# Moving one tile's transposes and norms inside the layer-1 out-projection of a two-layer trunk kernel

## The reference, cut to what matters

```
for each layer:
    sh1, sc1, g1, sh2, sc2, g2 = split(silu(cond) @ w_ada + b_ada)      # one set for the prompt, one for the sample
    h = rms_norm(x, g_norm1) * (1 + sc1) + sh1
    y = mixer(h) @ w_o            # layer 0: gated MLP and windowed attention; layer 1: latent attention, 16 heads
    x = x + g1 * y
    h = rms_norm(x, g_norm2) * (1 + sc2) + sh2
    x = x + g2 * hier_moe(h)      # 32 experts of width 256, 2 per token, chosen by a router
```

## Time and profile before

| what | value |
|---|---|
| median of 3 runs (lowest, highest) | 1056.43 us (1052.93, 1058.72) |
| the profiled execution's own time | 1052.93 us |
| its span in the trace | 1051.1 us |
| PE busy | 904.6 us, 86% of the span |
| DVE busy | 399.2 us, 38% |
| ACT busy | 239.1 us, 23% |
| POOL busy | 120.9 us, 12% |
| chain that ended last: PE, DMA, DVE, ACT | 60%, 24%, 10%, 3% |

### The profile page before, as it was taken

The page is one execution under the profiler, slowest core; times in us unless marked ns, Lnnn a source line. Parts: engine busy times, 40 slices in busy tenths (PEclk is TensorE's granted clock), DMA queues, the critical chain, the costliest instruction groups (busy, mean ns, idle before and its releaser), DMA issues.

```text
span 1051.1 us, 14384 instructions
## 1 busy us (share of the span) xinstructions
PE 904.6 (86%) x5389; PEld 518.8 (49%) x5389; DVE 399.2 (38%) x1155; ACT 239.1 (23%) x598; POOL 120.9 (12%) x131
## 2 busy tenths in 40 slices
PE   4899788995899988998769997998869998889880
PEld 1345336555555544555346663554555554545550
DVE  1102366234622233221163574662654222522114
ACT  3110134111011111111244444433201111111111
POOL 1000000100122212121100000001001222121210
PEclk9999999895999999999979998999879999999995
DMA  9979799357698999999761028107799899999974
GB/s 379 397 275 409 295 419 398 97 200 244 228 362 345 411 415 415 390 414 413 273 256 46 1 84 338 70 1 255 258 414 351 315 408 416 416 404 414 414 304 186
DMA packets 68717, 318.72 MB, mean 303 GB/s; under 512 B 12470, under 2 KB 13494, under 8 KB 45992
## 3 DMA queue, kind: packets, MB, share of 16 engines
q1 hardware_dynamic: 53184, 285.84, 68.5%
q0 software_dynamic: 13328, 25.02, 7.0%
q10 hardware_dynamic: 2144, 7.05, 1.7%
HBM read 312.72 MB, written 26.49 MB: 323 GB/s over the span
## 4 chain that ended last, share of the span: by engine, by line
PE 60%; DMA 24%; DVE 10%; ACT 3%; issue 2%; SPq 1%; POOL 0%; POOLq 0%; DVEq 0%; ACTq 0%
DMA ring<-in_l_w 17%; PE psum L783 13%; PE psum L986 7%; PE psum L796 7%; PE psum L733 4%; DMA ring<-in_l_w_ada 3%; PE psum L1203 3%; PE psum L1101 2%; PE psum L1042 2%; PE psum L1092 2%; PE psum L624 2%; PE psum L763 2%; PE psum L1133 2%; DMA scratch<-token_rows_hbm,overflow_rows 2%; PE psum L746 1%
## 5 line engine op out<-in xcount | busy, mean ns | idle before, releaser
L783 PE MATMUL psum<-ring,scratch 128*64 128x256 f32 x1920 | 225.4, 388 | 30.3 <-DMA ring<-in_l_w 28.7
L783 PEld LDWEIGHTS psum<-ring,scratch 128*64 128x64 f32 x1920 | 144.7, 139 | 96.0 <-issue 41.2
L1980 DVE TENSOR_TENSOR scratch<-scratch,psum 64x256 f32<-64x256 f32 x64 | 27.2, 425 | 306.6 <-ACT scratch L1350 302.3
L796 PE MATMUL psum<-ring,scratch 128*64 128x512 f32 x496 | 119.9, 604 | 2.6 <-ACT scratch L1354 1.9
L2437 POOL DMA_INDIRECT expert_rows<-scratch,slot_rows x64 | 63.9, 999 | 342.6 <-ACT scratch L1364 336.8
L1350 ACT ACTIVATE scratch<-psum 64x256 f32<-64x256 f32 x64 | 24.1, 377 | 265.5 <-PE psum L783 252.6
L986 PE MATMUL psum<-ring,scratch 128*128 128x512 f32 x192 | 74.8, 549 | 1.3 <-DVE scratch L2113 1.3
L1364 ACT COPY scratch<-psum 128x512 f32<-128x512 f32 x64 | 37.5, 587 | 145.4 <-PE psum L796 145.4
L624 PE MATMUL psum<-ring,scT 128*32 128x512 f32 x320 | 42.7, 657 | 15.8 <-DMA ring<-in_l_w_ada 14.7
L986 PEld LDWEIGHTS psum<-ring,scratch 128*128 128x128 f32 x192 | 36.8, 194 | 37.6 <-issue 36.5
L796 PEld LDWEIGHTS psum<-ring,scratch 128*64 128x64 f32 x496 | 31.2, 136 | 44.8 <-issue 39.8
(11 more groups left out here) (341 smaller groups left out, 1130.4 us busy)
## 6 DMA issues: line engine op xcount, KB each, us to landing
ring<-in_l_w SPq DMA_DIRECT2D x180, 1024.0 KB
ring<-in_l_w_ada SPq DMA_DIRECT2D x48, 1024.0 KB, 5.2
ring<-in_l_w_o SPq DMA_DIRECT2D x8, 1024.0 KB
ring<-in_l_w_in SPq DMA_DIRECT2D x4, 1024.0 KB
gate_rows<-gate_rows_hbm POOLq DMA_DIRECT2D x8, 512.0 KB, 7.4
scale_shift<-gate_rows_hbm POOLq DMA_DIRECT2D x8, 512.0 KB, 10.7
scratch<-expert_rows SPq DMA_DIRECT2D x8, 512.0 KB, 5.3
ring<-in_l_w_in SPq DMA_DIRECT2D x4, 768.0 KB
```

What stands on the lines that cost most here:

```text
L783: last = nc.tensor.matmul(ps[64 * n:64 * n + 64, 2 + par, 0:DE], mine[:, k, :], part(w, k * DE, DE), start=k == 0, stop=k == KD - 1)
L796: last = nc.tensor.matmul(ps[64 * n:64 * n + 64, 5 + par, :], hhT[:, par, k, :], part(w2, k * D + n * 512, 512), start=k == 0, stop=k == 1)
```

## The change

Nothing is computed otherwise. Two engines get another order in layer 1.

```diff
@@ PE
             weighted_values1(len(ATT1) - 1)
             project_sample(1)
+            transpose_h(3, hp, 0)
             project_sample(2)
-            transpose_h(3, hp, 0)
             transpose_h(3, hp, 1)
             router(1)
@@ DVE
             evac_out1(len(ATT1) - 1)
+            norm(3, 0)
             residual_sample(1)
-            norm(3, 0)
+            evac_h(3, h2T, 0)
             norm(3, 1)
+            evac_h(3, h2T, 1)
             residual_sample(2)
-            evac_h(3, h2T, 0)
-            evac_h(3, h2T, 1)
             norm(3, 2)
             evac_h(3, h2T, 2)
             router(1)
```

## The result

| what | before | changed |
|---|---|---|
| median, us (lowest, highest) | 1056.43 (1052.93, 1058.72) | 1066.03 (1061.56, 1070.63) |
| ratio to before, 95% interval | | 1.0105 [1.0079, 1.0132] |
| span of the profiled execution | 1051.1 | 1065.9 |

The change makes the kernel slower by 8.3 to 13.9 us. The changed kernel was measured a second time, with 1.0115 [1.0089, 1.0142]. The forecast of 1069.9 lies 3.9 us above the median and inside its range, and its 13.5 us lie inside the first interval, near the upper end. The two spans lie 14.8 us apart, more than the medians: 13.5 us of this arise in the stage, and 1.35 us are a later start of the out-projection, ahead of the change.

The account below looks back on a forecast made before the run. PE alone bounds the out-projection, then a relay starting with the residual of tile 2. Terms 8.7 + 0.95 + 2.2 + 1.7 = 13.5 us on the median 1056.43 give 1069.9 us; range 1063 to 1075 for 8 in 10.

Parts of the forecast that it names:

- The wait on PE: Between the out-projection's halves PE stops for tile 0's norm, which waits for scale and shift rows: 8.7 us, bounds 2.4 to 10.7.
- The transposes: Tile 0's eight transposes now stand ahead of the out-projection's second half on PE: 0.95 us.
- The clock: PE's clock falls to 1.2 GHz in the stop and stays low for 4.4 us afterwards: 2.2 us, bounds 0 to 2.6.
- The copies ahead of the residual: Tile 1's transposes and DVE's copy now precede the residual of tile 2: 1.7 us, bounds 1.5 to 2.0.
- The sum: Four terms delay the residual of tile 2 by 13.5 us, bounds 4.9 to 16.2.
- The rest gives nothing back: After the residual of tile 2, router and experts recover none of the 13.5 us; no gain counted.
- my bound: Sign in the expert stage: wrong on the weights' stream if PE's waits for weights fall by more than 3 us.
- The rule against it: Skill's GpSimd transfer estimate for the scale and shift rows: landed about 6.8 us after issue, no stop, sum 2.65 us.
- A (rows in time): Scale and shift rows land as in layer 0 or faster, shrinking PE's stop: say 4 us, 1060.4 us; chance 0.06.
- B (the stream pays back): Experts' waits for weights shrink by up to 13.5 us: 1056.4 us, chance 0.03; half of it 1063, chance 0.05.
- C (the clock holds): No clock fall in PE's stop: 11.3 us, 1067.7 us; chance 0.82 together with the forecast.
- D: SP's seven later ring loads delay expert 1, or low clock reaches the logits: up to 5 us more, 1075; chance 0.04.

Follow-up runs that it names:

- e4: Changed kernel plus nine unused 512-column matmuls in PE's stop, ahead of tile 0's transposes; stage 38.77 us, ratio to before 1.0113 [1.0068, 1.0158].
- e3: Changed kernel, but SP starts layer 1's five early expert loads only after the scale and shift rows landed; stage 37.20 us, ratio to before 1.0086.
- e1: Kernel before with only PE's part of the change, DVE in its old order; stage 39.55 us, ratio to before 1.0123 [1.0074, 1.0173].
- e9: Changed kernel unaltered, second profile and second comparison with before; stage 41.19 us, ratio to before 1.0115 [1.0089, 1.0142].
- e5: Changed kernel with tile 0's transposes moved inside the out-projection's second half, before its seventh of eight steps; stage 33.04 us, ratio to before 1.0036.
- e6: Kernel before plus 15 unused 512-column matmuls between the out-projection's halves; stage 42.62 us, ratio to before 1.0169 [1.0133, 1.0206].
- e8: As e7, plus eight unused matmuls ahead of layer 1's first transposes; stage 29.68 us, ratio to before 0.9963 [0.9934, 0.9992].
- e10: Kernel before unaltered, second profile; stage 27.84 us, ratio to before 0.9993 [0.9971, 1.0016].
- e7: Kernel before plus unused 512-column matmuls behind both routers' logits, three in layer 1, two in layer 0; ratio to before 0.9968 [0.9944, 0.9993].
- e2: Kernel before with only DVE's part of the change, PE in its old order; stage 35.47 us, ratio to before 1.0076 [1.0051, 1.0101].

## Why the prediction was right

The terms are read from start to start, with e4 for what the clock did: the stage of 41.32 us is 22.34 to the first transposes, 1.76 to the second half, 15.46 to the next transposes and 1.76 to the residual.

- *The wait on PE*, 8.7 us forecast: 8.34 us of idle time, and 8.55 us from start to start (22.34 less 13.79, half of the old block). The rows landed 15.9 us after their issue (16.0 in before), and the norm went no earlier though it now stood first. Right. e3 shows that 4.4 us of the landing go away with SP's loads and that 11.5 us do not; the lower bound of the term, 2.4 us by layer 0's landing, was too low for this place, where 3.97 was found.
- *The transposes*, 0.95 us: in e4, at the high clock, 0.93 us from their start to that of the second half. Right.
- *The clock*, 2.2 us: 2.55 us between the stages of the changed kernel and e4, 0.83 in the transposes and 1.72 in the second half. Right in mechanism, 0.3 us small. The clock fell 3.3 us into the idle time and not 4.7, and in e3 a stop of 4 us had it.
- *The copies ahead of the residual*, 1.7 us: 1.49 us, at the lower bound. The 1.77 us between the changed kernel and e1 look closer to the forecast, but hold 0.28 us of a shorter wait and a shorter second half in e1. Right in mechanism, 0.2 us large.
- *The sum*, 13.5 us in the stage: 13.48 us. That it agrees within 0.02 us is luck: the clock came out 0.3 us larger, the wait and the copies some 0.2 us smaller each. In the whole kernel 11.1 us [8.3, 13.9] and on the repeat 12.1 us [9.4, 15.0], whose centres lie 2.4 and 1.4 us under the forecast. Whether this is a difference can't be said from these intervals. e9 shows one thing that would make a part of it: a low clock at the end of attention, seen in 4 of 12 profiles (e5, e6, e8, e9), costs 1.8 us in before and nothing in the changed kernel. At that frequency it is some 0.6 us on average, an estimate from twelve profiles of ten kernels.
- *The rest gives nothing back.* The tails, 298.08 and 298.03 us, and e6 bear it out. PE's waits for weights in the late part fell from 14.6 us in 11 waits to 12.1 in 8. They are no good sign either way: in the second profiles they are 16.3 us (before, e10) and 15.1 us (changed, e9), so one kernel's value moves by up to 3 us, which is all of my bound.

```profile
...
PE psum L783 <- DMA ring<-in_l_w: 12.1, 8, 3.0
...
```

The fall to 12.1 has a cause of its own, and it is not the delay of 13.5 us. The same group of products, before and then changed:

```profile
...
931.61 3.67 PE L783 MATMUL psum<-ring,scale_shift 128*64 128x256 f32 x32 [0.92 <-DVE scale_shift L2056]
...
```

```profile
...
946.48 6.61 PE L783 MATMUL psum<-ring,scale_shift 128*64 128x256 f32 x32 [0.92 <-DVE scale_shift L2056]
...
```

Counted from the residual both begin at the same time, 181.6 and 181.7 us, so up to here nothing is given back. In the changed kernel the clock is at 0.56 over 945 to 950, the group takes 2.9 us longer, and the next ones run 3.0 us late. At 237 us after the residual the lag is down to 0.5 us, where before had waited 2.3 us for weights (at 977.93 and 986.53) and the changed kernel not at all, and at the end it is gone. So this late part does give back a delay of PE, but one that arises in it. The 13.5 us arise ahead of it and move the stream of weights as well, as the prediction had it.

- *The rule against it.* The estimate from the Trainium skill ("DMA: Bandwidth & Descriptors", section "Anatomy of one DMA — SWDGE (gpsimd) path") had the four rows landed 6.8 us after the first issue. The last of them took 11.5 us from its own issue even in e3, where SP's loads had not begun. The measurement decides: on this pattern, one row of HBM copied to 128 partitions four times, the estimate is far too short. e3's trace shows that the DMA engines were mostly busy in that time and moved little (a share of 0.82 at 152 GB/s); why this pattern moves so slowly was not tried.
- *The rivals.* A (rows in time) is out by the stop itself. B (the stream pays back) is out by e6 and by the experts' start times, which keep their distance from the residual. C (the clock holds) is out by the windows. D needed the seven loads to be missed, and PE has no wait for weights between the residual and 862 us.

## What to carry to other kernels

Before a wait is moved up in an engine's order, find when its signal was there and when the engine would now ask: here 744.6 and 736.0, which gives 8.6 us before anything else is counted, and the whole queue behind the wait pays it. Putting a norm first does not make it earlier when it waits for a transfer and not for its place. On TensorE add what the low clock costs after stops such as these, of 4 and 8 us: 2.55 us here. If the small work must move, put it at a point where its input is already there, as in e5, which took away two thirds of the loss. Filling the stop helps less: in e4 it brought back 2.55 us of the stage and nothing that the total shows, and in e7 1.7 of 2.9 us were lost again right behind the filled place. One lucky agreement is no check of a term: compare each with its own rows.

## What the hardware showed that I had not expected

- The clock at the end of attention differs between executions of the same code: 1.00 in the first profile of the changed kernel and low in the second, where the first half took 15.92 us instead of 14.00.
- The experts have such stretches too, at different places in different profiles: the same group of products takes 3.67 us or, with the clock low for a part of it, 5.36 (e3, e4, e6, e7). Most of what the tails of e3, e4 and e6 differ by is one or two of these groups.
- A fall of the clock came 3.3 us (changed), 2.9 us (e3) and 4.7 us (before) after the last matmul ended. After e2's single set of transposes it came at 753.5 (0.73 over 753 to 754), 2.5 us after their end.
- Four transfers of 512 KB, one row each copied to 128 partitions, with no load of SP beside them, still took up to 11.5 us from issue to landing in layer 1 (e3), and 9.9 in layer 0. In layer 0 the DMA share was 0.92 over 192 to 194 at 178 GB/s: the engines were busy and moved less than half of what they moved in other stretches.
